# Layer B with two groups in work at once, and the diagonal blocks of the key product copied by ScalarE

## The reference

```python
proj = h @ w_in                                   # q, k, v of all heads, gates
conv = silu(sum(xpad[:, wi:wi + T] * conv_w[wi] for wi in range(4)))
q, k, v = split(conv); q = l2norm(q) * SCALE; k = l2norm(k)
gc = cumsum(g)                                    # per chunk
decay = where(tri, exp(gc_i - gc_j), 0)
lmat = where(strict, (k * beta) @ k.T * decay, 0)
u, w = triangular_solve(I + lmat, [v * beta, k * beta * exp(gc)])
aqk = (q @ k.T) * decay
for each chunk:                                   # a recurrence over the chunks
    v_new = u - w @ S
    o = (q * exp(gc)) @ S + aqk @ v_new
    S = S * exp(g_last) + kdec.T @ v_new
```

## Time and profile before

| | |
|---|---|
| median of 3 runs | 2171.14 us (2170.03 to 2179.94) |
| the profiled execution | 2173.54 us, its span 2171.6 us |
| mean granted clock of PE over the span | 0.989 |
| PE busy | 2110.4 us (97%) |
| DVE, ACT, POOL busy | 986.9, 688.4, 450.8 us |
| layer B's projections, first to last unit | 1068.3 to 1732.8 us |

### The profile page before, as it was taken

One profiled execution on the slowest core, in us unless ns is written; L12 is line 12 of the kernel. 1 busy time (PEld: TensorE's weight loads), 2 busy tenths in 40 slices (PEclk: granted clock), 3 DMA queues, 4 the chain that ended last, 5 costly groups with the idle time before them and its releaser, 6 DMA issues.

```text
span 2171.6 us, 39599 instructions
## 1 busy us (share of the span) xinstructions
PE 2110.4 (97%) x16046; PEld 1508.9 (69%) x16046; DVE 986.9 (45%) x2521; ACT 688.4 (32%) x1615; POOL 450.8 (21%) x640
## 2 busy tenths in 40 slices
PE   8999999999999999999999999999998999999998
PEld 6888888888888876554566666666666666665444
DVE  5244354354344444321256666666666233333252
ACT  4122321312222131311145454444544344542101
POOL 0512231242124205000033312332231200020000
PEclk9999999999999999999999999999998999999999
DMA  7412201212221156777012212221110262124451
GB/s 234 151 41 67 81 26 46 78 40 56 74 59 42 30 183 226 228 220 219 23 57 92 75 74 86 74 85 76 59 42 13 62 269 82 39 74 140 135 167 53
DMA packets 210250, 210.53 MB, mean 97 GB/s; under 512 B 14262, under 2 KB 181654, under 8 KB 209151
## 3 DMA queue, kind: packets, MB, share of 16 engines
q1 hardware_dynamic: 198070, 148.27, 23.0%
q0 software_dynamic: 12000, 59.73, 7.1%
HBM read 179.56 MB, written 68.23 MB: 114 GB/s over the span
## 4 chain that ended last, share of the span: by engine, by line
PE 47%; DVE 3%; ACT 1%; issue 0%; DVEq 0%
PE bank L2093 17%; PE bank L2857 8%; PE bank L3347 7%; PE bank L2151 4%; PE bank L2167 2%; PE bank L2149 2%; DVE arena L2591 1%; PE bank L2159 1%; PE bank L2873 1%; PE bank L2882 1%; PE bank L3325 1%; PE bank L3358 0%; PE bank L2182 0%; PE bank L3254 0%; PE bank L3231 0%; ACT L2354 0%
## 5 line engine op out<-in xcount | busy, mean ns | idle before, releaser
L887 PE MATMUL bank<-arena 128*128 128x256 f32 (+1 forms) x2688 | 631.7, 386 | 0.0
L887 PEld LDWEIGHTS bank<-arena 128*128 128x128 f32 x2688 | 494.5, 190 | 75.3
L2093 PE MATMUL bank<-arena 128*128 128x352 f32 x1296 | 462.9, 474 | 0.1
L2093 PEld LDWEIGHTS bank<-arena 128*128 128x128 f32 x1296 | 219.8, 193 | 65.3 <-issue 0.6
L2857 PE MATMUL bank<-arena 128*128 128x352 f32 x576 | 176.4, 459 | 0.0
L3347 PE MATMUL bank<-arena 128*128 128x512 f32 x360 | 167.5, 599 | 0.0
L2151 PEld LDWEIGHTS bank<-arena 128*128 128x128 f32 x864 | 128.8, 196 | 42.9 <-DVE arena L2605 5.0
L2857 PEld LDWEIGHTS bank<-arena 128*128 128x128 f32 x576 | 106.6, 190 | 53.3
L2151 PE MATMUL bank<-arena 128*128 128x128 f32 x864 | 133.9, 282 | 3.8 <-DVE arena L2605 3.8
L1341 POOL TENSOR_TENSOR arena<-arena 128x272 f32<-128x272 f32 (+1 forms) x48 | 31.5, 656 | 507.9 <-ACT arena L1061 488.0
L1323 POOL TENSOR_TENSOR arena<-arena 128x512 f32<-128x512 f32 x96 | 122.7, 1278 | 10.9 <-POOL arena L1323 0.9
(11 more groups left out here) (430 smaller groups left out, 2783.7 us busy)
## 6 DMA issues: line engine op xcount, KB each, us to landing
arena<-in_w_in_a SPq DMA_DIRECT2D x48, 512.0 KB, 5.2
arena<-in_w_in_b SPq DMA_DIRECT2D x40, 512.0 KB, 5.1
arena<-in_cache_win_k SPq DMA_DIRECT2D x48, 256.0 KB, 6.2
arena<-in_cache_win_v SPq DMA_DIRECT2D x48, 256.0 KB, 4.7
out<-arena SPq DMA_DIRECT2D x40, 256.0 KB, 3.4
arena<-in_w_mem_kv SPq DMA_DIRECT2D x16, 512.0 KB, 8.1
arena<-in_cache_mem_k SPq DMA_DIRECT2D x32, 256.0 KB, 4.6
arena<-in_cache_mem_v SPq DMA_DIRECT2D x32, 256.0 KB, 3.8
```

What stands on the lines that cost most here:

```text
L887: m = nc.tensor.matmul(o[:, 0:hi - lo], w, y, start=k == 0 and i in (0, 1, 3, 5), stop=k == KH - 1, skip_group_check=i in (2, 4, 6))
L2093: m = nc.tensor.matmul(bank[j % 3][:, 0:PART], ring.slots[:, (B1 + b) % RING, k, :], part_in(k, part_), start=k == 0, stop=k == KD - 1)
```

## The change

The matrix steps of a group now reach over two passes of the loop. In pass G, slot 9 has ra of G and rl of G+1, and slot 11 has qk of G and kk of G+1 (`NEXT`); LT has a second buffer for that (`LTs`). ACT takes eight exponents in slot 9, G's and G+1's. In slot 11 ACT copies the diagonal blocks of G+1 out of LT (`choose_blocks`, four copies of 32 partitions x 112 elements), unmasked and without the first column of each block, in place of DVE's masked products. DVE spreads them in slot 13 (`base_rows(G + 1)`), does one base step in each of slots 14 and 15, and the other five in slots 0 to 3 of the next pass. The levels move up: level 3 to slots 4 and 5, level 4 to 6 and 7, level 5 to 10 and 12, level 6 to 13 and 14; kt goes to slot 6, vt to 15, the outputs of G-2 to 8. The SiLU of G+2's q and k goes to slots 12 and 13, that of v to slot 0 of the next pass; first taps and convolutions get other slots. Ahead of the loop, rl and kk of group 0 stand among the units, and its first two base steps ahead of slot 0. POOL's list stays as it is. The core of the diff:

```diff
-    picked = upper[:, 0:P].rearrange("p (c j b) -> p c j b", j=BASE, b=NBASE)
+    picked = upper[:, 0:4 * (BASE - 1) * NBASE].rearrange("p (c j b) -> p c j b", c=4, b=NBASE)
...
-    spread_rows = upper[:, 2176:2176 + 4 * BASE * 32]
+    spread_rows = upper[:, 2176:2176 + 4 * (BASE - 1) * 32]
+    LTs = [LT, upper[:, 3072:3584].rearrange("p (c e) -> p c e", e=P)]
...
+    PREP = {6: ("kt",), 9: ("ra", "rl"), 11: ("qk", "kk"), 15: ("vt",)}
+    NEXT = ("rl", "kk")
+    LEVEL_SLOTS = {(3, "x"): 4, (3, "z"): 5, (4, "x"): 6, (4, "z"): 7, (5, "x"): 10, (5, "z"): 12, (6, "x"): 13, (6, "z"): 14}
+    AT_ROWS = 13
+    STEPS_BEFORE = {14: 1, 15: 1}
+    STEPS = {0: 1, 1: 2, 2: 1, 3: 1}
+    NBS = 1 + 2 * (BASE - 1)
+    EARLY_STEPS = sum(STEPS_BEFORE.values())
+    AT_EXPS, AT_CHOICE = 9, 11
+    AT_SS, AT_ROOTS, AT_INV, AT_LOGS, AT_FACTORS, AT_OT = 3, 4, 5, 6, 7, 8
...
-    def p_names(s):
-        return PREP.get(s, ()) + ((level_name(*level_in[s]),) if s in level_in else ())
+    def p_names(G, s):
+
+        names = [(G + (n in NEXT), n) for n in PREP.get(s, ())]
+        if s in level_in:
+            names.append((G, level_name(*level_in[s])))
+        return [(g, n) for g, n in names if g < NG_]
...
     reader_of = lambda n: "act" if n == "ss" or n[:2] in ("qs", "tr") else "dve"
-    work = [(0, "ss")]
+    work = [(0, "ss"), (0, "rl"), (0, "kk")]
     for G in range(NG_ + 1):
         for s in SLOTS:
             if G < NG_:
-                work += [(G, n) for n in p_names(s)]
+                work += p_names(G, s)
...
-    TAP_AT = {3: 0, 8: 1, 11: 2}
-    conv_at = {4: (0, 1), 5: (0, 2), 7: (0, 3), 9: (1, 1), 11: (1, 2), 12: (1, 3), 13: (2, 1), 14: (2, 2), 15: (2, 3)}
-    silu_at = {7: 0, 12: 1, 15: 2}
+    TAP_AT = {0: 0, 4: 1, 11: 2}
+    conv_at = {1: (0, 1), 3: (0, 2), 4: (0, 3), 5: (1, 1), 7: (1, 2), 8: (1, 3), 12: (2, 1), 14: (2, 2), 15: (2, 3)}
+    silu_at = {12: 0, 13: 1}
...
                 readout(pe, g, f"zt{LEVELS - 1}")
-                if c:
-                    readout(pe, g, f"ks{c}")
+                readout(pe, g, f"ks{c}" if c else "vt")
...
+            unit(*u)
+        turned(0, "rl")
+        for u in units[PER_HEAD + KD:PER_HEAD + 2 * KD]:
+            unit(*u)
+        turned(0, "kk")
+        for u in units[PER_HEAD + 2 * KD:PER_HEAD + AHEAD]:
             unit(*u)
         for G in range(NG_ + 1):
...
+        def choose_blocks(G):
+
+            readout(act, G, "kk")
+            if G:
+                act.wait_ge(base, NBS * (G - 1) + 1)
+            for i in range(4):
+                q = quarter(i)
+                nc.scalar.copy(picked[q].rearrange("p c j b -> p c b j"),
+                               LTs[G % 2][q, :, q].rearrange("p c (b j) -> p c b j", j=BASE)[:, :, :, 1:]).then_inc(chosen, 1)
 
...
         silu(0, 2)
-        for i in range(3):
-            silu(1, i)
-        for u in ended(units[PER_HEAD:PER_HEAD + AHEAD]):
-            piece(*u)
+        first, second, third = ended(units[PER_HEAD:PER_HEAD + AHEAD])
+        piece(*first)
+        silu(1, 0)
+        exps(0, "rl", LT, 0)
+        piece(*second)
+        silu(1, 1)
+        choose_blocks(0)
+        silu(1, 2)
+        piece(*third)
         for G in range(NG_ + 1):
             for s in SLOTS:
                 if G < NG_:
-                    if s == 0:
-                        exps(G, "rl", LT, 0)
-                    elif s == 1:
+                    if s == AT_EXPS:
                         exps(G, "ra", AT, GR[G % 2][0])
+                        if G + 1 < NG_:
+                            exps(G + 1, "rl", LTs[(G + 1) % 2], 0)
+                    elif s == AT_CHOICE and G + 1 < NG_:
+                        choose_blocks(G + 1)
                 if s == AT_ROOTS:
...
+                if 0 < G < NG_ - 1 and s == 0:
+                    silu(G + 1, 2)
...
+        def turned(G, name):
+
+            h, cs = group(G)
+            lt, factors_of = LTs[G % 2], hd[:, h % 2]
+            b = left(dve, G, name)
+            if name == "rl":
+                nc.vector.tensor_tensor(lt, bk(b), wide4(mat(M_GT)), ALU.add).then_inc(rd_dve, 1)
+            elif name == "ra":
+                nc.vector.tensor_tensor(AT[:, cs, :], bk(b), wide4(mat(M_GE)), ALU.add).then_inc(rd_dve, 1)
+            elif name == "kk":
+                dve.wait_ge(exd, 2 * G + 1)
+                nc.vector.tensor_tensor(lt, lt, bk(b), ALU.mult).then_inc(rd_dve, 1)
...
-                    if t == 0:
-                        readout(dve, G, "kk")
-                        for i in range(4):
-                            q = quarter(i)
-                            nc.vector.tensor_tensor(picked[q].rearrange("p c j b -> p c b j"),
-                                                    LT[q, :, q].rearrange("p c (b j) -> p c b j", j=BASE),
-                                                    mats[q, M_HSEL, 4:4 + NBASE].unsqueeze(1).unsqueeze(3)
-                                                    .to_broadcast([32, 4, NBASE, BASE]), ALU.mult).then_inc(base, 1)
...
-        NBS = 5 + 2 * (BASE - 1)
-
         def base_rows(G):
 
-            dve.wait_ge(base, NBS * G + 4)
+            dve.wait_ge(chosen, 4 * (G + 1))
             nc.vector.tensor_copy(Md, mats[:, M_HSEL, 64:96].unsqueeze(1).to_broadcast([P, 4, 32]))
             nc.vector.transpose(spread_rows.rearrange("p (a b e) -> p a b e", b=NBASE, e=BASE),
                                 picked.rearrange("p c j b -> p (c j) b").unsqueeze(3)
-                                .to_broadcast([P, 4 * BASE, NBASE, BASE])).then_inc(base, 1)
+                                .to_broadcast([P, 4 * (BASE - 1), NBASE, BASE])).then_inc(base, 1)
 
         def base_step(G, n):
 
             j = BASE - 1 - n
-            done = NBS * G + 5 + 2 * n
-            rows_ = spread_rows.rearrange("p (c j b e) -> p c j b e", c=4, j=BASE, b=NBASE)[:, :, j, :, 0:j]
+            done = NBS * G + 1 + 2 * n
+            rows_ = spread_rows.rearrange("p (c j b e) -> p c j b e", c=4, b=NBASE, e=BASE)[:, :, j - 1, :, 0:j]
             m = Md.rearrange("p c (b e) -> p c b e", e=BASE)
             t = below.rearrange("p (c b) x -> p c b x", c=4)[:, :, :, 0:j]
             dve.wait_ge(base, done)
...
+                readout(dve, g, "vt")
...
-        for g in range(2):
-            for i in range(3):
-                for w in range(CW):
-                    conv(g, i, w)
-                if (g, i) == (0, 0):
-                    gate_sums_read()
-                if (g, i) == (0, 2):
-                    norm_inverses(0)
+        for i in range(3):
+            for w in range(CW):
+                conv(0, i, w)
+            if not i:
+                gate_sums_read()
+        norm_inverses(0)
+        for w in range(CW):
+            conv(1, 0, w)
         dve.wait_ge(ge, 3)
         head_terms()
         factors(0)
+        turned(0, "rl")
+        for w in range(CW):
+            conv(1, 1, w)
+        turned(0, "kk")
+        for w in range(CW):
+            conv(1, 2, w)
+        base_rows(0)
+        for n in range(EARLY_STEPS):
+            base_step(0, n)
         for G in range(NG_ + 1):
             for s in SLOTS:
                 if G < NG_:
...
-                if G < NG_ and s in BASE_STEPS:
-                    before = sum(n for t, n in BASE_STEPS.items() if t < s)
-                    if not before:
-                        base_rows(G)
-                    for n in range(before, before + BASE_STEPS[s]):
+                if G < NG_ and s in STEPS:
+                    first = EARLY_STEPS + sum(n for t, n in STEPS.items() if t < s)
+                    for n in range(first, first + STEPS[s]):
                         base_step(G, n)
-                    if s == BASE_END:
+                    if first + STEPS[s] == BASE - 1:
                         base_turned(G)
+                if G + 1 < NG_:
+                    if s == AT_ROWS:
+                        base_rows(G + 1)
+                    elif s in STEPS_BEFORE:
+                        first = sum(n for t, n in STEPS_BEFORE.items() if t < s)
+                        for n in range(first, first + STEPS_BEFORE[s]):
+                            base_step(G + 1, n)
                 if G + 2 < NG_ and s in conv_at:
                     conv(G + 2, *conv_at[s])
         out_factors(NG_ - 1)
```

More of the change, by code:

```diff
@@ L1989, in build @@
     (pd, pr_, wk, rd_act, rd_dve, cvd, sild, sqd, hdv, hda, exd, mt0, onm, sqo, fac, tails, sqrt_o, cstep, xzero,
-     cvs, spread, base, tap) = (
+     cvs, spread, base, tap, chosen) = (
         sem(f"b_{n}") for n in (
@@ L1994, in build @@
             "out_factors", "conv_tails", "out_roots", "conv_steps", "buffers_zeroed", "samples_convolved",
-            "diagonals_spread", "base_steps", "first_taps"))
+            "diagonals_spread", "base_steps", "first_taps", "blocks_chosen"))
     s_out = stored["state"]
@@ L2204, in chunk_step @@
                 to(g, f"su{c}", [(kdec[:, c, :], vn[:, c % 2, :])])
-        def matrix_step(G, s):
```

(52 more changed lines are left out.)

7 lines of the change are left out of this document (removed).

## The result

The changed kernel takes 2265.69 us (median of 4 runs, 2263.57 to 2266.80) against 2171.72 us for the kernel before in the same comparison: 1.0424 of it, with a 95% interval of 1.0396 to 1.0451. The forecast was 2266 us, with a range of 2222 to 2318, and slower. The profiled execution took 2266.48 us with a span of 2264.4; before it was 2173.54. So there are 92.9 us to be explained.

What follows compares the result with a forecast made beforehand. TensorE, busy nearly all the span, was taken as the bound, working down its slot list and waiting on other engines. Terms -24.4 - 1.9 - 8 + 87 + 13 + 28 + 1.4 = +95 gave a 2266 us median, range 2222 to 2318.

Steps and rivals of the forecast that it cites:

- waits for the base inverse: TensorE's 15 waits ahead of level 3 for the transpose ending the base inverse would go: -24.4 us.
- waits for r (L2605, now L2648): TensorE's two waits for DVE's r in the last groups would shrink: -1.9 us, between 0 and -3.8.
- hold at level 6: TensorE idles before level 6, as POOL's spread stands behind squares awaiting the later SiLU: 14 x 6.2 = +87 us.
- copy of tr behind eight exponents: TensorE in slot 10 waits for ACT's copy, behind eight exponents in slot 9: +13 us, bounds 0 and 20.
- lower clock: old part gone, new part: TensorE's half-clock stretches: half the old cost goes, -8 us; new ones behind 14 idle times cost 2 each, +28.
- rl ahead of the loop: At the start, the first rl stands 16 units ahead of the loop: +1.4 us, between 0 and 3.
- picks: DVE loses four instructions, 1.64 us a group, and ACT gets four copies, all off TensorE's path: 0 us.
- rival (b): On TensorE in layer B's loop, the clock never falls behind the new idle times: 2238 us; chance 0.13.
- (c): The clock stays at 0.5 for 10 us with TensorE back at work: 2310 us; chance 0.12.
- rival (a): At level 6, SiLU, squares and spread get through in time, so nothing holds TensorE: some 2151 us; chance 0.05.
- Rival (d): Level 3 still waits for the base inverse because ACT's copies or the steps come late: 2290 us; chance 0.04.
- Rival (e): ACT's table switch costs the chain before level 6 more than one load, 14 times: 2284 us; chance 0.04.

Runs made afterwards that it cites:

- exps_split_dve_picks: Changed kernel with POOL's spread ahead of the squares, ACT's exponents of G+1 one slot later, and VectorE's masked products in place of ACT's copies: 2146.62 us, 0.9853.
- spread_first: Changed kernel with one call moved in POOL's list, spread_diagonals(G) ahead of squares(G+2, 0): 2160.73 us, 0.9916 of the kernel before.

## Why the prediction was right

Beside each term, what the profile after shows:

| term | forecast | measured |
|---|---|---|
| waits for the base inverse | -24.4 | -24.4 (none left) |
| waits for r (L2605, now L2648) | -1.9 | -2.8 (3.8 to 1.0) |
| hold at level 6 | +87 | +86.6 |
| copy of tr behind eight exponents | +13 | +9.9 |
| lower clock: old part gone, new part | -8 + 28 = +20 | +17.7 |
| rl ahead of the loop | +1.4 | +1.2 |
| picks | 0 | 0 (by exps_split_dve_picks) |
| sum | +95 | +88.2 of 92.9 |

The clock's measured term adds up the stretches at 0.5 in the loop in which TensorE had matmuls running: 33.3 us before, 68.5 after, half of each, 16.6 and 34.3. Of the 92.9 us, 4.7 stay unassigned; 1.3 of them lie ahead of the loop (layer B's first unit starts at 1069.6, before at 1068.3).

**The deciding term** was right in place, count and size: 14 holds, 5.7 us idle in most of the even groups and 6.3 in the odd, and 8.1 in the last, G=13. That the total came out within 0.4 us is partly luck. All groups but the last were below the 6.0 and 6.5 us that were set, and G=13 made up for it. The parts of the chain erred both ways as well. The spread took 1.63 us, not 2.08 (the last section has the reason). ACT reached the copy of qs 1.32 us after the block's start in the instance above, an odd group, not 0.64: it had the piece's copy and the first tap ahead of it. I had put up to 0.4 us on that, and it was 0.7. ACT's four block copies also took 1.62 us where 1.2 to 1.5 were set, a bound drawn from 128x128 exponents and copies.

**The clock** fell at each of the 14 holds, as the forecast had it, which excludes rival (b). In the first two groups and the last it stayed at 0.5 for 10.2 us, in the others for about 6.8. In the holds' stretches, 3.6 to 6 us lay beside matmuls, and 6.8 in the last; that excludes (c). Half of them is 30.9 us, 2.2 for each hold, where 2 were set. Of the old term only two stretches of 3.4 us in the tail are left, so 13 us of it went, not 8. The two misses run against each other, and the net term came out 2 us lower.

**The other side**, rival (a), was decided at the point that was named: it needed less than 1.4 us idle at level 6 in a group, and there were 6.2. With the hold taken away, spread_first is faster than the kernel before by 0.84%, 17.8 us on its chip, where rival (a) had 20 us or 0.9%. Its sum was sound as well, and it was the order of POOL's list that did not let it happen; its terms were less so, as the copy of tr cost 16.1 us there and not 13. Rival (d) fell with the vanished waits for the base inverse.

**Rival (e)**, a change of tables that costs more than its load, falls by the timeline: the load starts 0.01 us behind the copy's end and the next activation 0.01 us behind the load's. The Trainium skill, "ScalarE: Activation LUTs", section "What ACT_TABLE_LOAD costs", adds a drain of about 1.38 us to it; in this kernel's rows there is none beside the 1.28 us.

**The term that was off most** is the copy of tr: 9.9 us, and 16.1 without the hold, where 13 were set for both. The last three groups came to 5.2 us, as set, but the twelve full ones waited 0.39 us each, not 0.65. These are also below the 0.5 to 2 us that were named as a sign. The term was taken as independent of the hold, and it is not.

## What to carry to other kernels

When a step is moved to a later slot, look through the lists of all engines that wait for it, and at what stands behind the waiting instruction: here a 1 us product that nobody needed soon, waiting for its own input, held a 2 us copy that everybody needed, and one call moved in POOL's list was worth 5%. A wait of 6 us on TensorE cost about 8.4 here (86.6 us idle and 30.9 of clock over 14), as the granted clock is down when work goes on. Off-loading an engine that is not the bound (1.6 us a group from VectorE to ScalarE) gave nothing.

## What the runs showed of the hardware that was not expected

The same spread on POOL ran faster in the changed kernel. The view by line and shape (mean duration in ns behind the total) of the kernel before, and of the changed one:

```profile
L2769 POOL TENSOR_TENSOR arena<-arena 128x256 f32<-128x256 f32 x16 | 12.9, 805 | 25.5 <-DVE arena L2557 25.5
```

```profile
L2826 POOL TENSOR_TENSOR arena<-arena 128x256 f32<-128x256 f32 x16 | 9.9, 618 | 4.8 <-DVE arena L2601 4.8
```

The mean of 805 ns hides two kinds. In the kernel before, ten of the sixteen took 618 to 620 ns, beside other work of DVE or none, and six took 1062 to 1151. These six are the ones that began while a tap of DVE's convolution (L2458) was running, with 584 to 672 ns of it to go. It goes the other way too: a tap that began during the spread's second instruction took 1.3 us in most cases, in place of 0.74. Both, in the timeline of the kernel before:

```profile
1283.14 1.64 POOL L2769 TENSOR_TENSOR arena<-arena 128x256 f32<-128x256 f32 x2 [0.64 <-DVE arena L2557]
1284.00 1.32 DVE L2458 SCALAR_TENSOR_TENSOR arena<-arena 128x512 f32<-128x512 f32 x1
...
1321.44 0.74 DVE L2458 SCALAR_TENSOR_TENSOR arena<-arena 128x512 f32<-128x512 f32 x1
1321.51 2.17 POOL L2769 TENSOR_TENSOR arena<-arena 128x256 f32<-128x256 f32 x2
```

The 2.08 us of the earlier trace rows, which the forecast took for every group, are a case by itself: the tap began within the spread's first instruction, and the second then took 1508 ns, where it mostly took 1052 to 1060. In the changed kernel DVE stood idle for POOL during nearly every spread, so none was slowed; in spread_first (625 ns in the mean) DVE was at work, but none of its taps was running when a spread began. The Trainium skill, "GPSIMD Engine Reference", section "1. Specifications", says that the two engines share their SBUF interfaces and that DVE instructions with two SBUF inputs contend. The trace agrees: the tap reads both of its inputs from SBUF, and the scaling L2508, which reads its data from a bank, ran beside all ten quick spreads at its usual 0.75 us.

The clock fell less readily than waits alone suggest. In spread_first TensorE waits for the copy of tr in each full group, 0.39 to 1.23 us, and the granted clock is full from the loop's start until G=13, where it falls behind two waits of 1.56 and 2.4 us. In the kernel before, with a wait of 1.5 to 1.7 us in nearly every full group, it fell once in them, behind one of 1.72 us; four more waits of 1.72 or 1.73 us left it full. What decides between one wait of 1.7 us and the next was not looked into.
